# A hybrid decoder trunk in fp32 pairs: the conformer taps moved to one engine, its LayerNorm moved into attention

## What is computed

```python
z = rmsnorm(x) @ W_in            # columns in four groups A, B, C, D
A: y = B_gate * causal_dwconv3(C_gate * h)
B: u = a * sigmoid(g)                                   # 256 channels
   u = causal_dwconv(u, w_conv) + b_conv                # 31 taps
   y = silu(layernorm(u, ln_g, ln_b))                   # over the 256 channels
C: MoBA attention, 4 heads of 64, causal, softmax
D: MLA attention: q latent 384 and kv latent 128, each RMS-normed and projected
   up, 4 heads of 64 + 32 rotary
x = x + rmsnorm(concat(A, B, C, D) @ W_out)
x = x + rmsnorm(conv_ffn(rmsnorm(x)))                   # gated, hidden 2816, 3 taps
```

## Time and profile before

| | |
|---|---|
| median of 3 runs | 1291.93 us (1291.92 to 1294.03) |
| profiled execution | 1295.56 us, span 1293.8 us |
| mean granted TensorE clock | 0.969 |
| busy share: TensorE, VectorE, ScalarE, GpSimd | 95%, 66%, 46%, 18% |
| conformer taps on VectorE (L1042) | 60 instructions, 72.9 us busy |
| conformer additions on GpSimd (L774) | 60 instructions, 98.1 us busy |

### The profile page before, as it was taken

One profiled execution on the slowest core, in us unless ns is written; L12 is line 12 of the kernel. 1 busy time (PEld: TensorE's weight loads), 2 busy tenths in 40 slices (PEclk: granted clock), 3 DMA queues, 4 the chain that ended last, 5 costly groups with the idle time before them and its releaser, 6 DMA issues.

```text
span 1293.8 us, 15712 instructions
## 1 busy us (share of the span) xinstructions
PE 1230.5 (95%) x6036; PEld 1033.4 (80%) x6036; DVE 858.3 (66%) x1306; ACT 592.1 (46%) x889; POOL 233.8 (18%) x208
## 2 busy tenths in 40 slices
PE   5997999999999999999999799989899999999997
PEld 5885867878888888888898687778788888888885
DVE  4699577577666666544769977675676666665463
ACT  3453367454444444434545534664454444444432
POOL 1284166120000000000006733551100000000000
PEclk9998988999999999999999999599999999999999
DMA  7222202353333333466632231024333333335563
GB/s 234 78 66 82 75 1 72 122 153 91 95 96 95 96 97 97 152 193 209 197 98 77 65 92 33 1 83 163 114 114 98 97 96 94 96 98 186 181 216 126
DMA packets 155677, 143.18 MB, mean 111 GB/s; under 512 B 6447, under 2 KB 137427, under 8 KB 155603
## 3 DMA queue, kind: packets, MB, share of 16 engines
q1 hardware_dynamic: 154480, 140.40, 35.6%
q10 hardware_dynamic: 1123, 1.79, 0.4%
HBM read 140.07 MB, written 2.10 MB: 110 GB/s over the span
## 4 chain that ended last, share of the span: by engine, by line
PE 79%; DVE 13%; POOL 3%; issue 2%; DMA 2%; ACT 1%; SPq 0%; POOLq 0%; DVEq 0%; ACTq 0%
PE ps L461 26%; PE ps L462 25%; PE ps L463 25%; DVE cf_out L1042 4%; DVE wsp L393 2%; PE ps L672 2%; POOL prob L807 1%; POOL rms_r L765 1%; DMA x<-in_x 1%; DVE xn L883 1%; DVE rot L939 1%; DMA raw<-in_w_ffn_up 1%; DVE hid L944 1%; DVE shuf L937 1%; PE ps L516 1%
## 5 line engine op out<-in xcount | busy, mean ns | idle before, releaser
L461 PE MATMUL ps<-xn,wsp 128*128 128x512 f32 (+2 forms) x1136 | 422.5, 372 | 21.0 <-DVE xn L883 15.7
L462 PE MATMUL ps<-xn,wsp 128*128 128x512 f32 (+2 forms) x1136 | 419.3, 369 | 0.0
L463 PE MATMUL ps<-xn,wsp 128*128 128x512 f32 (+2 forms) x1136 | 419.1, 369 | 0.0
L393 DVE TENSOR_TENSOR wsp<-raw,wsp 128x1024 fp32r<-128x1024 f32 (+2 forms) x250 | 307.8, 1233 | 160.2 <-ACT wsp L385 160.1
L385 ACT ACTIVATE wsp<-raw 128x1024 fp32r<-128x1024 f32 (+1 forms) x256 | 266.9, 1043 | 186.9 <-PE ps L463 151.0
L461 PEld LDWEIGHTS ps<-xn,wsp 128*128 128x128 f32 (+1 forms) x1136 | 217.0, 191 | 59.4 <-DVE xn L883 17.9
L462 PEld LDWEIGHTS ps<-xn,wsp 128*128 128x128 f32 (+1 forms) x1136 | 216.9, 191 | 35.2 <-issue 0.5
L463 PEld LDWEIGHTS ps<-xn,wsp 128*128 128x128 f32 (+1 forms) x1136 | 216.7, 191 | 35.5
L461 PE MATMUL ps<-wsp,hid 128*128 128x512 f32 (+1 forms) x488 | 189.9, 389 | 0.0
L463 PE MATMUL ps<-wsp,hid 128*128 128x512 f32 (+1 forms) x488 | 189.3, 388 | 0.0
L462 PE MATMUL ps<-wsp,hid 128*128 128x512 f32 (+1 forms) x488 | 189.3, 388 | 0.0
(11 more groups left out here) (138 smaller groups left out, 1395.6 us busy)
## 6 DMA issues: line engine op xcount, KB each, us to landing
raw<-in_w_ffn_up SPq DMA_DIRECT2D x88, 512.0 KB, 3.8
raw<-in_w_ffn_down SPq DMA_DIRECT2D x88, 512.0 KB, 4.3
raw<-in_w_in SPq DMA_DIRECT2D x40, 512.0 KB, 3.9
raw<-in_w_out SPq DMA_DIRECT2D x32, 512.0 KB, 3.4
x<-in_x SPq DMA_DIRECT2D x4, 512.0 KB, 9.6
out_x<-x SPq DMA_DIRECT2D x4, 512.0 KB, 4.1
raw<-in_w_uq SPq DMA_DIRECT2D x4, 288.0 KB, 3.0
gain_mix<-in_norm_mix_post SPq DMA_DIRECT2D x2, 512.0 KB, 4.9
```

What stands on the lines that cost most here:

```text
L393: eng.tensor_tensor(wsp[:, u % SPLIT, 1, 0:nk * n], raw[:, (l * NU + u) % RAW, 0:nk * n], fp(wsp[:, u % SPLIT, 0, 0:nk * n]), ALU.subtract ...
L461: pe.matmul(dst, a[0], b[0], start=start, stop=False, skip_group_check=True)
L462: pe.matmul(dst, a[0], b[1], start=False, stop=False, skip_group_check=True)
L463: return pe.matmul(dst, a[1], b[0], start=False, stop=stop, skip_group_check=True)
```

## The change

All 62 taps of a layer are VectorE instructions; ScalarE's products, GpSimd's additions, `cf_tmp` and the semaphore `cf_prod` are gone. A tap of half 0 and one of half 1 alternate (`conv_taps`), and `CF_VECTOR` counts such pairs: one in step 3, none in 4 to 7, then one to three in each step up to 20 except 19. Seven pairs lie behind the loop: two in step 20 behind its last product, two behind the third key part of MLA, three behind the values' parts and ahead of the query parts. LayerNorm moves: the mean's matmuls into TensorE's attention step 1, the centring into step 2, the squares into ScalarE's steps 3 and 4, their addition into GpSimd's step 4, the statistics into TensorE's step 6, the variance and the power into step 7, the broadcast into step 9, the scaling into step 10, gain, bias and tanh into 11 and 12, swish into 13 to 15 and the lo part into 17 and 18. `cf_u`, `cf_th` and the squares (`ln_sq`, in place of the shared `sq`) lie in the slots of the conformer's own result.

```diff
-CF_VECTOR = {3: 2, 4: 1, 5: 1, 6: 1, 7: 1, 8: 4, 9: 4, 10: 4, 11: 2, 12: 4, 13: 4, 14: 3}
-CF_SCALAR = {3: 1, **{g: 3 for g in range(4, 14)}}
+CF_VECTOR = {3: 1, 8: 2, 9: 2, 10: 2, 11: 1, 12: 3, 13: 2, 14: 3, 15: 3, 16: 1, 17: 2, 18: 2, 20: 2, 21: 2, 22: 3}
...
-        cf_u = place("cf_u", [P, 2, T + CF_TAPS - 1], f32, slot(VL))
+        cf_u = place("cf_u", [P, 2, T + CF_TAPS - 1], f32, slot(Y_SLOT["b"]))
...
-        cf_th = place("cf_th", [P, 2, T], f32, slot(Y_SLOT["c"]))
+        cf_th = place("cf_th", [P, 2, T], f32, slot(Y_SLOT["b"] + 1))
...
-        cf_tmp = place("cf_tmp", [P, 2, T], f32, slot(CQN + 2))
+        ln_sq = place("ln_sq", [P, 2, T], f32, slot(Y_SLOT["b"]))
...
@@ TensorE
-                    if g == 19:
-                        pe.wait_ge(cf_conv, l + 1)
-                        pe.wait_ge(cf_sum, (l + 1) * (CF_TAPS - 1))
-                        pe.wait_ge(lat_norm, l * 4 + 4)
-                        for c in range(2):
-                            last = pe.matmul(ps[:, STAT, :], ones[:, :], cf_out[:, c, :], start=c == 0, stop=c == 1)
-                        last.then_inc(mean_done, 1)
...
-                    if h == 1:
-                        stat("ln", l)
...
-                    if t == 2:
+                    if t == 1:
+                        pe.wait_ge(cf_conv, l + 1)
+                        pe.wait_ge(cf_sum, (l + 1) * CF_TAPS)
+                        for c in range(2):
+                            last = pe.matmul(ps[:, STAT, :], ones[:, :], cf_out[:, c, :], start=c == 0, stop=c == 1)
+                        last.then_inc(mean_done, 1)
+                    if t == 6:
+                        stat("ln", l)
+                    if t == 9:
                         spread("ln", l)
                     if TRAIL <= t < N_ATT + TRAIL:
                         transposes(t - TRAIL)
...
@@ GpSimd
-                for j in range(1, CF_TAPS):
-                    pool.wait_ge(cf_prod, l * CF_TAPS + j + 1)
-                    if j > 1:
-                        pool.wait_ge(cf_sum, l * (CF_TAPS - 1) + j - 1)
-                    pool.tensor_tensor(cf_out[:, 1, :], cf_out[:, 1, :], cf_tmp[:, j % 2, :], ALU.add)\
-                        .then_inc(cf_sum, 1)
...
-                sums("ln", l)
...
-                rsqrt("ln", l)
...
                     if t in (1, 4):
                         query_sum({1: 2, 4: 3}[t])
+                    if t == 4:
+                        sums("ln", l)
+                    if t == 7:
+                        rsqrt("ln", l)
...
@@ VectorE
+                def conv_taps(g):
+                    for _ in range(CF_VECTOR.get(g, 0)):
+                        j = cf_taken[0]
+                        cf_taken[0] += 1
+                        if j == 0:
+                            own(glu_done, l * 2 + 2)
+                            ins = dve.tensor_scalar(cf_out[:, 0, :], cf_u[:, 0, 0:T], col(l, "conv_b", 0),
+                                                    col(l, "conv_b_bias", 0), ALU.mult, ALU.add)
+                        else:
+                            st.wait()
+                            ins = dve.scalar_tensor_tensor(cf_out[:, 0, :], cf_u[:, 0, j:j + T],
+                                                           col(l, "conv_b", 2 * j), cf_out[:, 0, :],
+                                                           ALU.mult, ALU.add)
+                        if j == CF_TAPS - 1:
+                            ins.then_inc(cf_conv, 1)
+                        else:
+                            st.mark(ins)
...
+                            own(cf_sum, l * CF_TAPS + j)
+                            ins = dve.scalar_tensor_tensor(cf_out[:, 1, :], cf_u[:, 1, j:j + T],
+                                                           col(l, "conv_b", 2 * j + 1), cf_out[:, 1, :],
+                                                           ALU.mult, ALU.add)
+                        ins.then_inc(cf_sum, 1)
...
                     dve.tensor_tensor(ml_k[h][0:DH, 1, :], ps[0:DH, bank_of(G_MK + h), :], fp(ml_k[h][0:DH, 0, :]),
                                       ALU.subtract).then_inc(kn_ready, 1)
+                    if h == 2:
+                        conv_taps(G_MK)
...
+                conv_taps(G_MK + 1)
...
                     if t == 2:
+                        dve.wait_ge(mean_done, l + 1)
+                        for c in range(2):
+                            dve.scalar_tensor_tensor(cf_out[:, c, :], ps[:, STAT, :], -1.0 / GW, cf_out[:, c, :],
+                                                     ALU.mult, ALU.add).then_inc(cf_cent, 1)
+                    if t == 7:
+                        event_var("ln", l)
+                    if t == 10:
                         scale_ready("ln", l)
...
-                    if t in (5, 6):
-                        c = t - 5
+                    if t in (13, 14):
+                        c = t - 13
...
-                    if t in (9, 10):
-                        c = t - 9
+                    if t in (17, 18):
+                        c = t - 17
...
@@ ScalarE
-                    for _ in range(CF_SCALAR.get(g, 0)):
...
-                    if g == 20:
-                        for c in range(2):
-                            act.wait_ge(cf_cent, l * 2 + c + 1)
-                            square("ln", c, cf_out[:, c, :], l)
...
                     if t in (3, 4):
                         c = t - 3
+                        act.wait_ge(cf_cent, l * 2 + c + 1)
+                        square("ln", c, cf_out[:, c, :], l)
+                    if t in (11, 12):
+                        c = t - 11
                         act.wait_ge(cf_norm, l * 2 + c + 1)
...
-                    if t in (6, 7):
-                        c = t - 6
+                    if t in (14, 15):
+                        c = t - 14
```

More of the change, by code:

```diff
@@ L118, in rms_no @@
     return TC + l * 16 + stage * 8 + RMS_ORDER.index((what, c))
-CF_VECTOR = {3: 2, 4: 1, 5: 1, 6: 1, 7: 1, 8: 4, 9: 4, 10: 4, 11: 2, 12: 4, 13: 4, 14: 3}
-CF_SCALAR = {3: 1, **{g: 3 for g in range(4, 14)}}
-assert sum(CF_VECTOR.values()) == CF_TAPS and sum(CF_SCALAR.values()) == CF_TAPS
+CF_VECTOR = {3: 1, 8: 2, 9: 2, 10: 2, 11: 1, 12: 3, 13: 2, 14: 3, 15: 3, 16: 1, 17: 2, 18: 2, 20: 2, 21: 2, 22: 3}
+assert sum(CF_VECTOR.values()) == CF_TAPS
 N_ATT = 2 * HEADS * TC
@@ L559, in stat @@
                 for c in range(TC):
-                    last = pe.matmul(ps[:, STAT, c:c + 1], sq[:, 0, c * P:(c + 1) * P], ones[:, 0:1],
+                    last = pe.matmul(ps[:, STAT, c:c + 1], (ln_sq if ev == "ln" else sq)[:, 0, c * P:(c + 1) * P], ones[:, 0:1],
                                      start=True, stop=True)
@@ L1033, in _ @@
                                .then_inc(sc_val, 1)
[L1034 to L1048 removed]
+                    conv_taps(g)
                 own(sc_val, l * 2 + 2)
```

43 lines of the change are left out of this document (8 added, 35 removed).

## The result

| | before | after |
|---|---|---|
| median of 6 runs | 1291.93 us | 1302.78 us (1300.12 to 1305.21) |
| ratio | | 1.0081, 95% interval 1.0070 to 1.0092 |
| profiled execution, its span | 1295.56, 1293.8 us | 1304.43, 1302.6 us |
| mean granted clock | 0.969 | 0.963 |

What follows compares the result with a forecast made beforehand. TensorE, busy for 95% of the span, was taken to bound the kernel. Layer 0 at +0.8 and layer 1 at +1.8 us, with the credit about +2, gave 1297.5 against the profiled execution, 1294 as a median; range 1280 to 1303.

Steps and rivals of the forecast that it cites:

- A: The forecast itself: the whole kernel at 1290 to 1298 us, chance 0.50.
- rival C: Slower: thin opening plus step 6 wait hold attention's clock at 0.50 until the MLA heads; 1303 us, chance 0.15.
- Part 1: In-projection: all taps on VectorE, TensorE's two waits go; gain 14.4 us in layer 0, 13.4 in layer 1.
- Rival D: VectorE not relieved: taps cost 0.78 us or more, in-projection keeps a wait; +6 us, 1300, chance 0.08.
- Part 2: Seven tap pairs behind group 20: last product to first mask takes 20.5 us, 6.5 more than before.
- Part 3, step 6: Attention: statistics wait 4.3 us for GpSimd's addition of the squares, then run 0.8 to 1.6 us; 5.9 us taken.
- GpSimd's lag: GpSimd's four rope instructions end behind the first mask, a lag carried into the fourth product; 0.6 us.
- The broadcast (step 9): Attention: broadcast waits for GpSimd's power, bounds 0.9 to 5 us; 2.2 taken, as products run ahead of TensorE.
- LayerNorm's rest (steps 10 to 18): Attention, under TensorE's low stretch: costs nothing if the clock is still low, about 1 us a layer if not.
- The clock: Attention: low stretch of 20 to 35 us a layer; 1 us credited in all for low time spent in waits.
- What a low microsecond costs: Attention: each microsecond at the lower clock level loses about 0.45 us.
- Rival B: Faster: low stretch in attention shrinks, as TensorE rests early and finds dense work afterwards; 1282 us, chance 0.27.

Runs made afterwards that it cites:

- experiment 8: Kernel before without GpSimd's 30 additions a layer, so half 1 keeps only its first tap (work left out); 1273.38 us in one run.
- experiment 2: Changed kernel with its seven late pairs of taps moved to step 18 or earlier, LayerNorm still in attention; 1289.28 us, ratio 0.9975.
- experiment 5: Changed kernel with unread matmuls: 12 before the mean, 16 before the statistics, five each in steps 4, 5 and 8; 1295.23 us, ratio 1.0034.
- experiment 9: experiment 1 plus unread matmuls in attention: three a step in steps 4 to 7, 1268.24 us; five, 1258.92; three in steps 3 to 15 (long), 1277.87.
- experiment 4: Changed kernel with unread matmuls, six in front of the mean and eight in front of the statistics; 1295.06 us, ratio 1.0022.
- experiment 1: Kernel before with all taps on VectorE in alternating pairs, done by step 18, LayerNorm left in its old place; 1273.08 us, ratio 0.9828.
- experiment 7: experiment 6 with LayerNorm's broadcast in step 11 instead of 9 and what hangs on it two steps later; 1277.10 us, ratio 0.9874.
- experiment 6: experiment 2 with both squares in ScalarE's step 3 and GpSimd's addition directly behind prob(3); 1280.80 us, ratio 0.9907.

## Why the prediction was off, and by which step

The forecast was 1294, the median is 1302.78, 8.8 above it: outside A's own range, and 0.2 us inside the wide one, whose upper end was rival C's 1303. The six runs go from 1300.12 to 1305.21, so that the wide range held its median is luck.

**Part 1 held.** No wait of TensorE at all from 60 to 145 us, clock 1.00, taps 0.66 us apart where 0.67 was said, group 20 earlier by 14.8 and 14.3 us where 14.4 and 13.4 were said. Rival D is out. The reason given, VectorE late because of GpSimd's additions, was tested by itself (experiment 8).

**Part 2 held up to 0.9 us.** 21.4 us from group 20 to the first mask, where 20.5 were said, in both layers. Missing was one wait: the third query part needs the slot of `ml_shuf` that GpSimd's first rope sum gives back, 1.55 us at 165.39. The prediction had seen GpSimd's four rope instructions as late and took them for a matter of the fourth product only; the next consumer stood in VectorE's own queue, ahead of the mask. The seven pairs by themselves cost 13.5 us (experiment 2), for a group 20 that ends 1.6 us earlier in sum.

**Part 3, step 6, held in mechanism.** The wait is 4.1 us (4.3 said), with the queue as told, and the statistics 1.87 us (1.6 said). Masks 0 to 8 grew by 4.8 us a layer, less than the 6.5 with GpSimd's lag. TensorE was not full there before either: the transposes had waited 0.98 us.

**Behind mask 8 three terms were too small**, and that is the missing time. The sum had +1.6, the account has +8.9, 7.3 more: 10.0 more behind mask 8, 1.9 more in front of the first mask, 3.3 less in masks 0 to 8, and 1.2 more gain in the in-projections (rounded). Behind mask 8 the sum had 2.2 a layer for the broadcast less 1 for the clock, 3.4 in all; the account has 13.4.

- *The broadcast (step 9), 2.2 us.* The wait is 1.2 us, under the 2 that were said, but masks 8 to 12 grew by 4.1 and 2.5. All of masks 8 to 12 was low before, and in after all in layer 0 (hence 4.1) and 7.3 us in layer 1. At the full clock, and with filler in both, the difference is the same: 11.6 us in experiment 5, 7.6 in experiment 9. "The products run ahead of TensorE" was true of GpSimd's queue and said nothing of ScalarE, which stands still for 4.9 us at the same broadcast (experiment 4).
- *LayerNorm's rest (steps 10 to 18), "nothing if it is still low, about 1 us a layer if not".* Nothing was put in the sum; masks 12 to 31 took 4.1 us more over both layers, at the same low time in them (17.9 us, before 18.2). The table has masks 12 to 31 in us, by the low time in them; experiments 1 and 2 differ only in LayerNorm's place:

| low time in masks 12 to 31 | LayerNorm done before | LayerNorm's rest among them |
|---|---|---|
| 0 | 29.2, 29.2 (experiment 9, five) | |
| 2.9 to 3.4 | 31.3 (before, layer 0), 31.5 (experiment 1, layer 1) | 34.9 (after, layer 1), 34.9, 34.9 (experiment 4) |
| 6.8 | | 34.9 (experiment 2, layer 0), 34.9, 34.9 (experiment 5) |
| 14.5 to 15.3 | 35.7 (before, layer 1), 35.5 (experiment 1, layer 0) | 36.2 (after, layer 0), 36.2 (experiment 2, layer 1) |

```profile
199.30:230.60 31.30, 28.94 (x197) 24.77 (x196) 24.29 (x121) 23.98 (x67) 21.75 (x24) 0.95 0.25 85
828.60:864.30 35.70, 33.83 (x197) 29.66 (x195) 24.65 (x120) 23.96 (x67) 21.77 (x24) 0.79 0.21 75
```

  These rows are before; those of after stand above. Where the clock is low the work costs 0.5 to 0.8 us, nearly the "nothing" that was said; where it is high it costs 3.4 to 3.6 us, not 1. VectorE and ScalarE are each some 3 us busier there and TensorE only 28.9 of 34.9 us.
- *The clock.* The prediction credited 1 us, and expected 20 to 35 us low in a layer; it was 47.8 and 30.7. But the 24 us more lie in masks 0 to 8, where the account is under the forecast, and not behind mask 8. What the clock did add lies on the way to the FFN in layer 1: 2.7 us longer, with 6.8 us low at 925.4 where before has none.

The medians differ by 10.9, 2 more than the profiles, because before's profiled execution was slower than its median by 3.6 and after's by 1.7.

**Rival C** named the right time, 1303, and nearly the right low time: 24 us more where it had 25, its mark of 60 us passed. Its price was 0.45 us for each, "or less where TensorE waits anyway". TensorE does wait there, the time came from elsewhere, and the agreement is in the main luck. Nor did the low clock hold to the start of the MLA heads in both layers: in layer 1 it ended at 829.8, between masks 8 and 12.

**What a low microsecond costs** was 0.45 in the prediction. By the table it is 0.43 in masks 12 to 31 without LayerNorm (35.5 for 29.2, 14.7 us low) and 0.12 to 0.17 with it (36.2 for 34.9, 11.1 or 7.7 us more low). Over both openings experiment 9 bounds it: 58 low us against none are 14.3 us, with 40 filler matmuls in the way, which take 1.44 us for five, 11.5 in all and partly in waits. That makes 14.3 / 58 = 0.25 to 25.8 / 58 = 0.44. So 0.45 is the upper end, and a stretch in which other engines bound too loses less.

**Rival B** had the lever right and the sign of this case wrong. It expected TensorE to rest early and find dense work afterwards; here steps of small matmuls follow the wait, and the low stretch grew. Where matmuls of 128x512 were put in, low time was less (experiments 4, 5, 9).

**Idle gaps and the clock.** The rule of the Trainium skill ("TensorE: Matmul & The Clock Gate", Why this matters for your kernels), by which idle gaps throw the clock back and steady work restores it, explains only part of this. In experiment 1 the clock fell with no wait above 0.7 us and stayed low for 34.1 us at 33.6 busy.

**What stays open:** what makes the clock fall and come back where it does; why the long filler of experiment 9 didn't hold it; what the last 4.0 us of experiment 7 over experiment 1 are; and how much of the gain of experiment 6 is wait and how much is clock, since no run changed one without the other.

## What to carry to other kernels

Before moving work, ask what stands where it goes: the LayerNorm that took TensorE 1.7 us for the mean and no wait in a dense stretch cost 8 us a layer in a ring of small steps (experiment 2 against 1). Price such a move on every engine of the ring and not by TensorE's wait alone, and compare stages at equal granted clock: at equal clock the work that the forecast had put at nothing is plain. Where a wait is put into an in-order queue, read the releasing engine's queue backwards and move the releasing instruction to the front before accepting the wait; that was worth 8.5 us here. And where the granted clock is low although the engine is busy, try filler before rearranging, and in more than one dose: 40 unread matmuls gave 14 us, 78 gave nothing.

## What the runs showed of the hardware that was not expected

- TensorE stayed at 0.50 for 34.1 us while busy for 33.6 of them, and for 47.8 us in after; in the second layer of after it came back after 27.3 us, between masks 8 and 12, so neither a step nor an elapsed time fixes the end.
- The price of low clock depended on what else bounds a stretch: masks 4 to 8 took 9.4 us with 7.1 to 9.4 us of it, and with none and filler among them; masks 12 to 31 lost 6.3 us to 14.7 of it, and with LayerNorm among them 1.3 us to 11.1.
- The clock fell in experiment 1 at 168.3, after no wait above 0.7 us, 5.8 us behind the first mask.
- Twenty added matmuls a layer, 5.8 us of work, made the openings 9.1 and 5.2 us shorter; with twelve, two runs of six were as fast.
- The low stretches of one program came back in the same places, within 0.5 us, in another profile, while two programs that differ by 40 matmuls have 0 and 58 us of them.
- Independent taps on VectorE start 0.66 us apart though each lasts 0.74; while GpSimd added, the same instruction took 1.2 us.
